# Expert blocks of 32 places instead of 64, with the next block's rows turned behind W2 of the block before

## The reference, cut to what matters

```python
# xt: 1024 tokens x 1024; w1, w3: 32 experts x 1024 x 512; w2: 32 x 512 x 1024
gsel = argmax(xt @ w_group + b_group)             # one of 4 groups of 8 experts
ev, ei = top_k(expert logits of that group, 2)    # two experts a token
ew = softmax(ev) * gprob[gsel]
# the 2048 (token, expert) pairs are sorted by expert
y = (silu(xb @ w1[e]) * (xb @ w3[e])) @ w2[e]     # for the rows xb of each expert e
out = sum over a token's two experts of ew * y
```

## Time and profile before

| | |
|---|---|
| median of 3 runs | 1649.77 us |
| the profiled execution | 1650.04 us |
| its span (first to last instruction) | 1648.4 us |
| mean granted TensorE clock | 0.988 |
| PE busy | 1564.9 us, 95% |
| DVE busy | 560.9 us, 34% |
| ACT busy | 346.8 us, 21% |
| POOL busy | 300.6 us, 18% |
| DMA | 328.42 MB, mean 199 GB/s |

### The profile page before, as it was taken

One profiled execution on the slowest core, in us unless ns is written; L12 is line 12 of the kernel. 1 busy time (PEld: TensorE's weight loads), 2 busy tenths in 40 slices (PEclk: granted clock), 3 DMA queues, 4 the chain that ended last, 5 costly groups with the idle time before them and its releaser, 6 DMA issues.

```text
span 1648.4 us, 21863 instructions
## 1 busy us (share of the span) xinstructions
PE 1564.9 (95%) x7698; PEld 848.1 (51%) x7699; DVE 560.9 (34%) x1542; ACT 346.8 (21%) x859; POOL 300.6 (18%) x431
## 2 busy tenths in 40 slices
PE   7999998999999999998999999799899999999986
PEld 4554544444444444444444555566466666666652
DVE  4210004766566656654222354511011111111115
ACT  3000002443343443433000111111111111111113
POOL 2000001322222222222001001221121212121114
PEclk9999999999999999998999999999999999999997
DMA  9214621553111110103443821699999989999928
GB/s 236 67 56 62 125 78 58 166 181 114 45 32 26 45 33 26 46 13 90 161 136 103 357 107 74 235 416 419 419 419 418 386 352 407 416 421 417 415 85 306
DMA packets 135914, 328.42 MB, mean 199 GB/s; under 512 B 40046, under 2 KB 80398, under 8 KB 126640
## 3 DMA queue, kind: packets, MB, share of 16 engines
q1 hardware_dynamic: 117472, 297.98, 49.5%
q0 software_dynamic: 9984, 17.62, 3.2%
q10 hardware_dynamic: 8400, 12.07, 2.1%
HBM read 276.09 MB, written 55.25 MB: 201 GB/s over the span
## 4 chain that ended last, share of the span: by engine, by line
PE 83%; DVE 7%; DMA 5%; issue 2%; ACT 2%; POOL 1%; SPq 1%; POOLq 0%; ACTq 0%; DVEq 0%
PE PS L856 17%; PE PS L707 12%; PE PS L591 11%; PE PS L870 9%; PE PS L745 7%; PE PS L780 7%; PE PS L693 4%; PE PS L654 4%; PE PS L673 4%; PE PS L586 3%; DMA WA<-w 2%; PE PS L833 2%; DMA BA<-hn_d,ids 1%; POOL WA L1532 1%; PE PS L573 1%
## 5 line engine op out<-in xcount | busy, mean ns | idle before, releaser
L707 PE MATMUL PS<-WA 128*128 128x512 f32 x512 | 255.0, 611 | 2.2 <-ACT WA L967 1.6
L856 PE MATMUL PS<-WA,BA 128*64 128x256 f32 x2048 | 227.6, 379 | 2.9 <-DMA WA<-w 1.5
L856 PEld LDWEIGHTS PS<-WA,BA 128*64 128x64 f32 x2048 | 173.9, 137 | 63.9 <-issue 17.3
L591 PE MATMUL PS<-WA,BA 128*128 128x512 f32 x416 | 180.1, 593 | 2.9 <-DVE WA L1090 2.9
L1450 POOL TENSOR_SCALAR BA<-BA,rin,gates 128x640 f32<-128x640 f32 (+7 forms) x128 | 99.6, 781 | 270.8 <-DVE rin L1209 270.8
L1364 DVE SCALAR_TENSOR_TENSOR BA<-BA,PS 128x256 f32<-128x256 f32 x46 | 19.4, 422 | 340.8 <-ACT BA L1029 340.8
L591 PEld LDWEIGHTS PS<-WA,BA 128*128 128x128 f32 x416 | 78.6, 190 | 99.6 <-issue 96.2
L673 PEld LDWEIGHTS PS<-ident,BA 128*128 128x128 f32 x648 | 79.4, 144 | 94.1 <-issue 86.6
L870 PE MATMUL PS<-WA,BA 128*64 128x512 f32 x512 | 116.9, 597 | 9.7 <-DVE BA L1374 8.7
L707 PEld LDWEIGHTS PS<-WA 128*128 128x128 f32 x512 | 84.6, 190 | 78.4 <-issue 67.6
L957 ACT ACTIVATE BA<-PS,ngm 128x640 f32<-128x640 f32 (+7 forms) x128 | 89.9, 702 | 130.5 <-DVE ngm L1187 126.1
(11 more groups left out here) (249 smaller groups left out, 1548.4 us busy)
## 6 DMA issues: line engine op xcount, KB each, us to landing
WA<-w SPq DMA_DIRECT2D x66, 2048.0 KB, 25.3
BA<-w SPq DMA_DIRECT2D x30, 2048.0 KB, 27.6
rows_d<-WA SPq DMA_DIRECT2D x8, 2048.0 KB, 9.5
rows_d<-BA ACTq DMA_DIRECT2D x92, 128.0 KB, 6.8
WA<-w_in SPq DMA_DIRECT2D x16, 512.0 KB, 5.6
gates_d<-WA SPq DMA_DIRECT2D x32, 256.0 KB, 2.4
WA<-gates_d SPq DMA_DIRECT2D x8, 1024.0 KB, 5.4
BA<-w_in SPq DMA_DIRECT2D x26, 256.0 KB, 6.1
```

The lines of the kernel that those rows point to most:

```text
L591: mm = pe.matmul(PS[:, j % 4, :], ws[:, c % 6, k, :], hnT[:, k, 512 * h:512 * h + 512], start=(k == 0), stop=(k == KT - 1))
L707: mm = pe.matmul(PS[:, 6, :], gw[:, j, k, :], hnT[:, k, 512 * hf:512 * hf + 512], start=(k == 0), stop=(k == KT - 1))
L856: mm = pe.matmul(PS[DH * h:DH * h + DH, bank, 0:256], xT[:, k, :], w[par][:, k, 256 * h:256 * h + 256], start=(k == 0), stop=(k == KT - 1))
```

## The change

`SLOTS` is 32 instead of 64, and an expert has at least 2 blocks (of 32) instead of 1 (of 64). The total is rounded up to an even number, because ACT, DVE and POOL now handle blocks in pairs (`side` 0 and 1). The parts:

- W1 and W3 run in four column groups of 32: two for the halves of W1, two for those of W3, all in bank 0, one after the other in the innermost loop. They share one semaphore, `mm13`. W2 runs in four column groups with 256 output columns each.
- The order on TensorE: W1 and W3 of block b, W2 of block b - 1 (`put_out`), the transposes of the rows of block b + 1 (`next_rows`), the transpose of the hidden rows of block b (`turn_hidden`). The first block of an expert is written apart from its loop, since its `put_out` uses the weights of the expert before.
- The gather brings 32 whole rows into 32 partitions of one of two buffers (`rows_in`). DVE spreads them over 128 partitions with four copies (`spread_rows`), so that two transposes turn them.
- Row numbers are read two blocks ahead, one DMA a block instead of two; the table holds token numbers instead of half-row numbers.
- ACT copies the output in four pieces and stores it with one DMA a block, from one of two buffers.
- The first two blocks' numbers both come from `first_rows`; `mark`, its matmuls and the gather behind them are gone. The first block's rows are turned by 8 transposes straight from the gathered rows.

```diff
-SLOTS = 64
-MAXB = NE + 2 * SEQ // SLOTS
+SLOTS = 32
+MAXB = 2 * NE + 2 * SEQ // SLOTS - 4
+FIRST = 2 * SLOTS
...
# SP
-                sp.wait_ge(S[("mm1", "mm3", "y_ps")[j]], used)
+                sp.wait_ge(S[("mm13", "mm13", "y_ps")[j]], used)
...
# TensorE
-            for m in range(TT):
-                for c in range(2):
-                    for h in range(2):
-                        mm = pe.matmul(PS[DH * h:DH * h + DH, 2, 0:2], mark[:, m, c, :], tok[:, h, m, :], ...)
         def turn_rows():
-            for c in range(4):
+            for c in range(2):
                 mm = pe.transpose(PS[:, 7, P * c:P * c + P], xin[:, P * c:P * c + P], ident[:, :])
...
+        def hidden_sums(b, par, landed):
+            pe.wait_ge(S["xT_evac"], pe.snap(b + 1))
+            for n in range(2):
+                pe.wait_ge(S[f"we{3 * par + n}"], landed)
+            for k in range(KT):
+                for q in range(4):
+                    w = (W1, W3)[q // 2][par]
+                    mm = pe.matmul(PS[SLOTS * q:SLOTS * q + SLOTS, 0, 0:256], xT[:, k, :],
+                                   w[:, k, 256 * (q % 2):256 * (q % 2) + 256], start=(k == 0), stop=(k == KT - 1))
+            mm.then_inc(S["mm13"], 1)
+        def next_rows(b):
+            pe.wait_ge(S["x_free"], pe.snap(b + 2))
+            turn_rows()
+        def put_out(n_done, par, landed):
+            pe.wait_ge(S["hT_done"], n_done)
+            pe.wait_ge(S["y_evac"], n_done)
+            pe.wait_ge(S[f"we{3 * par + 2}"], landed)
+            for j in range(2):
+                for h in range(2):
+                    for n in range(4):
+                        mm = pe.matmul(PS[SLOTS * n:SLOTS * n + SLOTS, 3, 0:256],
+                                       hT[:, FIRST * j + SLOTS * h:FIRST * j + SLOTS * h + SLOTS],
+                                       W2[par][:, 2 * h + j, 256 * n:256 * n + 256], ...)
+            mm.then_inc(S["y_ps"], 1)
+        def turn_hidden(b):
+            pe.wait_ge(S["hid_done"], pe.snap(b + 1))
+            pe.transpose(PS[:, 2, 0:P], hv, ident[:, :]).then_inc(S["hT_ps"], 1)
+        def expert(e, lo, par, landed, landed_before):
+            hi = pe.value_load(starts_i[0:1, bass.ds(e + 1, 1)], ...)
+            hidden_sums(lo, par, landed)
+            if landed_before is not None:
+                put_out(lo, (par - 1) % NW, landed_before)
+            next_rows(lo)
+            turn_hidden(lo)
+            with pe.Fori(lo + 1, hi) as b:
+                hidden_sums(b, par, landed)
+                put_out(b, par, landed)
+                next_rows(b)
+                turn_hidden(b)
+            return hi
...
# ACT
         def gate_and_rows(b):
-            act.wait_ge(S["mm1"], b + 1)
-            nc.scalar.activation(th[:, :], PS[:, 0, 0:256], ACT.Tanh, scale=0.5)...
-            act.wait_ge(S["x_tr"], b + 3)
-            act.wait_ge(S["mm3"], b + 1)
+            act.wait_ge(S["mm13"], b + 1)
+            nc.scalar.activation(th, PS[0:FIRST, 0, 0:256], ACT.Tanh, scale=0.5)...
+            act.wait_ge(S["x_tr"], b + 1)
             nc.scalar.copy(xT_out, xT_ps).then_inc(S["xT_evac"], 1)
+        def put_rows(n_done, side, first):
+            act.wait_ge(S["y_ps"], n_done)
+            for n in range(4):
+                y = nc.scalar.copy(ysb[side][:, 256 * n:256 * n + 256], PS[SLOTS * n:SLOTS * n + SLOTS, 3, 0:256])
+            y.then_inc(S["y_evac"], 1)
+            act.wait_ge(S["y_evac"], n_done + 1)
+            act.dma_start(rows_d[bass.ds(first, SLOTS), :], ysb[side]).then_inc(S[f"y_st{side}"], 16)
+        with act.Fori(1, act.snap(total - 1), 2) as b:
+            for n in range(2):
+                gate_and_rows(act.snap(b + n + 1))
+                act.wait_ge(S[f"y_st{1 - n}"], act.snap(b * 8 + 8 + 16 * n))
+                put_rows(act.snap(b + n + 1), 1 - n, act.snap((b + n) * SLOTS))
...
# DVE
-        step(dve.tensor_scalar(nblk_i, cnt_i, 6, None, ALU.arith_shift_right))
-        step(dve.tensor_scalar(sums[0][:, 16:48], nblk_i, 1, None, ALU.max))
+        step(dve.tensor_scalar(nblk_i, cnt_i, 5, None, ALU.arith_shift_right))
+        step(dve.tensor_scalar(sums[0][:, 16:48], nblk_i, 2, None, ALU.max))
...
+        def spread_rows(side):
+            for q in range(4):
+                rows = dve.tensor_copy(xin[SLOTS * q:SLOTS * q + SLOTS, :], rows_in[side][:, 256 * q:256 * q + 256])
+            rows.then_inc(S["x_free"], 1)
...
+        with dve.Fori(0, total, 2) as b:
+            for side in range(2):
+                now = dve.snap(b + side)
+                hidden(now)          # mm13, tanh: the product, then two halves of 64 partitions
+                dve.wait_ge(S[f"x_blk{side}"], dve.snap(b * 8 + 32))
+                dve.wait_ge(S["x_tr"], dve.snap(b + side + 1))
+                spread_rows(side)
+                take_hidden(now)     # one copy of 128 columns
...
# POOL
+        def load_ids(side, row):
+            pool.dma_start(ids[0:SLOTS, side:side + 1], ids_d[bass.ds(row, SLOTS), 0:1], ...)
+        with pool.Fori(2, total + 2, 2) as b:
+            for side in range(2):
+                pool.wait_ge(S[f"ids_in{side}"], pool.snap(b * 8))
+                pool.wait_ge(S["x_free"], pool.snap(b + side - 1))
+                pool.wait_ge(S[f"x_blk{side}"], pool.snap(b * 8))
+                ...
+                g.indirect_dma_start(rows_in[side], None, hn_d[:, :], ...)
+                load_ids(side, pool.value_load(block_row_i[0:1, bass.ds(b + side + 2, 1)], ...))
```

More of the change, by code:

```diff
@@ L248, in build @@
     ZPARTS = 8
+    ZROWS = MAXB * SLOTS * D // (512 * P)
     steps_at, tile_done_at = [], {}
@@ L875, in _ @@
-        with pe.Fori(0, NE // NW) as e3:
+        def hidden_sums(b, par, landed):
+            pe.wait_ge(S["xT_evac"], pe.snap(b + 1))
+            for n in range(2):
+                pe.wait_ge(S[f"we{3 * par + n}"], landed)
+            for k in range(KT):
+                for q in range(4):
[3 more added lines that the diff above has]
+            mm.then_inc(S["mm13"], 1)
@@ new lines, in next_rows @@
+        def next_rows(b):
[8 more added lines that the diff above has]
+                    for n in range(4):
+                        mm = pe.matmul(PS[SLOTS * n:SLOTS * n + SLOTS, 3, 0:256], hT[:, FIRST * j + SLOTS * h:FIRST * j + SLOTS * h + SLOTS],
+                                       W2[par][:, 2 * h + j, 256 * n:256 * n + 256],
+                                       start=(j == 0 and h == 0), stop=(j == 1 and h == 1))
+            mm.then_inc(S["y_ps"], 1)
@@ L876, in _ @@
+        end = pe.snap(pe.value_load(starts_i[0:1, 0:1], min_val=0, max_val=0))
+        for e in range(NW):
+            end = expert(e, end, e, 16, None if e == 0 else 16)
+        with pe.Fori(1, NE // NW) as e3:
+            end = pe.value_load(starts_i[0:1, bass.ds(e3 * NW, 1)], min_val=2, max_val=MAXB)
             for par in range(NW):
-                expert(e3 * NW + par, e3 + 1, par)
+                end = expert(e3 * NW + par, end, par, pe.snap(e3 * 16 + 16), pe.snap(e3 * 16 if par == 0 else e3 * 16 + 16))
@@ L878, in _ @@
+        end = pe.value_load(starts_i[0:1, NE - NE % NW:NE - NE % NW + 1], min_val=2, max_val=MAXB)
         for e in range(NE - NE % NW, NE):
-            expert(e, e // NW + 1, e % NW)
+            end = expert(e, end, e % NW, 16 * (e // NW + 1), 16 * ((e - 1) // NW + 1))
+        put_out(end, (NE - 1) % NW, 16 * ((NE - 1) // NW + 1))
         pe.wait_ge(S["loop_left"], 1)
@@ L1285, in place @@
                 dve.wait_ge(S["first_ps"], 1)
-                dve.tensor_scalar(ids[:, 2:3], PS[:, 0, 0:1], PS[:, 0, 1:2], None, ALU.add).then_inc(S["first_ids"], 1)
+                for n in range(2):
+                    rows = slice(SLOTS * n, SLOTS * n + SLOTS)
+                    dve.tensor_scalar(ids[0:SLOTS, 2 + n:3 + n], PS[rows, 0, 0:1], PS[rows, 0, 1:2], None, ALU.add) \
+                        .then_inc(S["first_ids"], 1)
             step(dve.tensor_reduce(slot_f[:, m, :], pick, X, ALU.add))
@@ L1500, in _ @@
         scatter_ids(TT - 1)
[L1501 to L1504 removed]
         pool.wait_ge(S["scattered"], 16 * 2 * TT)
[L1507 to L1511 removed]
+        def load_ids(side, row):
+            pool.dma_start(ids[0:SLOTS, side:side + 1], ids_d[bass.ds(row, SLOTS), 0:1],
+                           allow_slow_non_contiguous=True).then_inc(S[f"ids_in{side}"], 16)
```

210 lines of the change are left out of this document (80 added, 130 removed).

## The result

The changed kernel takes 1659.9 us (median of 3 runs, 1659.83 to 1661.95), the kernel before 1649.77: a ratio of 1.0065, 95% interval 1.0051 to 1.0078. It is slower by 0.65%; the forecast was 1622.0 us, 1.7% faster. The profiled execution has a span of 1657.9 us at a mean clock of 0.975.

What follows compares the result with a forecast made beforehand. TensorE set the loop, with the weights' stream close behind as the next wall. From 1650.0 us, 29 off the loop, 0.5 off before it and 0.9 more after gave 1621, stated as 1622; range 1606 to 1656.

Steps and rivals of the forecast that it cites:

- The stream of weights: In the expert loop, 199.5 MB at 414.5 GB/s take 481 us, so the last W2 lands at about 1549.
- except at the start ... I count 1 us: At the loop's start, the third block's numbers wait for the row table: 1 us; first weight slot free at 1067.
- the 2 us that I had put in: In the loop, 2 us added for the granted clock falling after TensorE's waits.
- 78 blocks, the last eight experts among them: Loop count: 78 blocks of 32 instead of 46 of 64; the last eight experts need 22 blocks.
- W1 and W3 four abreast: In each block, 64 instructions in four column groups run four at 0.216 us: 3.45 us, last sum at 3.61.
- the rivals of the groups: In W1, W3 and W2, four column groups don't run abreast: 1700 to about 2000 us; chance 0.16, loads included.
- of the loads: Rival in the column-group matmuls: weight loads can't hide, a block takes 9.5 us, about 1840 us; chance 0.02.
- The chain of ACT and DVE under W2 of the block before: In each block, hidden rows are ready at 5.03 us, covered by the previous block's W2 until 5.18; period 6.4 us.
- The rival of the handshakes: In each block, waits before W1 and late rows cost more: period 7.0 to 7.3 us, 1640 to 1665; chance 0.09.
- The first block 0.5 us earlier: Before the loop, marks and 32 small matmuls go, rows' landing sets ACT's copy: 0.5 us earlier taken.
- Waits of some 4 us for weights, a share of DMA at 1.0 until 1550 and a granted clock under 1.00: Signs of a right forecast in the loop: such waits with most two-block experts, and the low clock in these stretches.
- The stream runs faster: Rival for the loop's weight stream: fewer small packets worth 2% of the rate, 9 us less, 1612; chance 0.09.

Runs made afterwards that it cites:

- Experiment 4: The changed kernel with each loop gather's 32 whole rows put into partitions 0, 4, ..., 124 (1627.7 us) or 0, 2, ..., 62 (1656.8 us).
- experiment 5: The kernel before with each loop gather split into two of 64 half rows, into partitions 0 to 63 and 64 to 127: 1672.4 us, ratio 1.0145.
- Experiment 6: The changed kernel with the last row-number scatter moved earlier (1660.2 us), or the third expert's W2 (1657.8) or W3 and W2 (1653.9) held for the third block's rows.
- e11: The changed kernel with rows gathered into partitions 0, 4, ..., 124 and the third expert's W3 and W2 held until the third block's rows landed: 1621.8 us.
- e1: The changed kernel without the gathers of rows from the third block on: 1614.3 us, ratio 0.9788.
- e4: The changed kernel with GpSimd's last scatter of row numbers put before the second of the two first gathers: 1660.2 us, ratio 1.0059.
- e9: The changed kernel with the third expert's W3 and W2 issued only when the third block's rows have landed: 1653.9 us, ratio 1.0021.
- e2: The changed kernel with rows gathered as quarters of 1 KB into 128 partitions instead of 32 whole rows into 32: 1632.3 us, ratio 0.9895.
- e5: The changed kernel with each loop gather's 32 whole rows put into partitions 0, 4, ..., 124 instead of 0 to 31: 1627.7 us, ratio 0.9864.

## Why the prediction was wrong

The step that failed is "The stream of weights": 199.5 MB at the 414.5 GB/s of the earlier trace rows. I took a rate measured in the kernel before as a property of the transfers, and carried it over a change of the gathers' destination. It had 128 partitions to write and got 32. At 393 GB/s the same 199.5 MB take 508 us, 26 us more. Experiment 4 shows the cause by one changed line, experiment 5 by the gathers alone in the kernel before. That the row gathers keep the weights' transfers waiting is shown by the share of q1 and by the packets, 0.75 us instead of 0.62 (experiment 4); how the partitions are tied to the path is not to be seen in a trace. A rule that fits stands in the Trainium skill (SBUF — State Buffer, section "Door 1: The DMA port swizzle"): bits 4 to 2 and bit 6 of a partition's number choose one of 16 ports, so partitions 0 to 31, 0 to 63 and 0, 2, ..., 62 all reach the same 8, and 0, 4, ..., 124 all 16. All runs here agree with it: 390 to 398 GB/s for the first three, 420 to 422 for the last. The section speaks of the bandwidth of the transfer itself, here 8 MB of rows; what it cost was the rate of the weights beside them. The same skill (DMA: Bandwidth & Descriptors, "Back-pressure in remote DMA") says that a clogged port stalls the other queues of the engine that writes to it. It says so of transfers between cores; the packets here fit it for one core's own, but no trace shows the stall itself.

The second failed term is small in the text: "except at the start ... I count 1 us". The first slot was free at 1074.7, not 1067: 7.7 us. I had the latencies of small transfers behind full queues (7.4 and 8.0 us) and used them inside the loop only; and I did not ask what stands behind DVE's wait for rows. Experiment 6 gets 6 us of it back.

26 + 7.7 = 34 of the 39 us between the forecast loop end (1574) and the measured one (1612.9). Over the whole stream, 1075 to 1580 us, the rate was 391, which makes it 29 + 7.7 = 37; the other 2 are open. With both causes removed the time is 1621.8 us. That it agrees with 1622.0 so well is in part luck: that run's rate is 421, not 414.5, worth 8 us, so something else in the loop is 8 us longer than I worked out. Its trace says where. The last eight experts start at 1426.8, after 4.36 us of waiting for weights; by the sum at 421 GB/s these are there at about 1421. And the 22 blocks from there, with the last W2, take 147.1 us and not 144: one W1 and W3 at a low clock takes 6.33 us instead of 3.66, two waits that the trace puts down to nothing take 1.9 and 1.4, and the first block of an expert mostly comes 0.3 us late. Over the loop the clock costs more than the 2 us that I had put in: L843 is busy for 206.0 + 89.5 = 295.5 us in e11 where 78 x 3.66 are 285.5. But only 2.7 of these 10 us lie in the last 22 blocks, where TensorE sets the time. Why the weights of the last eight come 6 us later than by the sum stays open.

The other steps:
- 78 blocks, the last eight experts among them: right.
- W1 and W3 four abreast: right, 3.66 us for 3.61, so the rivals of the groups and of the loads (slower) fall. The rule of the Trainium skill (TensorE: Matmul & The Clock Gate, "Part 3: Packing small matmuls — row/col tiling") that weight loads overlap running matmuls only where the row group differs went with 1840 us in the prediction. The trace disagrees with it: 64 loads of 114 ns lie within those 3.66 us.
- The chain of ACT and DVE under W2 of the block before: right. Period 6.22 us for 6.4, ACT's copy L1050 as the last releaser, its wait 0.35 us. The rival of the handshakes falls.
- DVE's spreading: 1.18 us, inside 0.8 to 1.7, and free; ACT's four copies 1.49 for 1.5.
- The first block 0.5 us earlier: can't be told. The loop began at 1049.12 for 1050.42, but among the profiled runs of variants that change nothing ahead of it the same point moves by 5 us (1048.7 in e11, 1054.1 in e1).
- Waits of some 4 us for weights, a share of DMA at 1.0 until 1550 and a granted clock under 1.00 were named as what would show the forecast right. All came, and said nothing of the rate: I should have named GB/s. Neither sign of being wrong came, a period over 7 us or a share well under 1.0.
- The rival of the stream looked one way only. "The stream runs faster" got 0.09; that it might run slower had no case and no chance, though its price per GB/s stood in the sum: 1.2 us each, and the forecast gain of 28 us is gone at 24 GB/s less, 390.

The chances followed: 0.20 for slower, all of it on TensorE. The half about TensorE, with all its detail, was right, and it decided nothing once the bound had moved.

## What to carry to other kernels

When a change hands the bound from an engine to the transfers, the rate of the transfers has to be costed like an instruction: list every transfer that runs beside the stream, and ask for each whether its destination, partition by partition, changes. Small gathers that land in partitions 0 to 31 or 0 to 63 took 6% off the rate of the weights in flight beside them; the same rows over all 128 partitions, or one in every four, took 1% or nothing. And a small transfer on the path (scatter, numbers, rows) that meets megabytes of prefetch took 8 us instead of under 4. To put it first in the queue only made the next small transfer late (e4); holding the prefetch until all of them were through got 6 us back (e9).

## What the runs showed of the hardware that was not expected

- Matmuls of 32 columns of weights and 256 columns of data in four column groups: 64 instructions with their 64 loads in 3.66 us, against 7.11 for 64 in two groups. Four abreast cost nothing over two.
- A gather of 0.13 MB a block, about 4% of the bytes, into partitions 0 to 31 or 0 to 63 slows the weights, 92% of the DMA engines' time, by 6%, and the row stores out to memory not at all. The share of DMA stays at 1.02; only GB/s shows it.
- 64 destinations (0 to 63) are no better than 32 (0 to 31): 390 to 393 against 391 to 396 GB/s.
- Spaced destinations are even better than 1 KB quarters over all partitions: 420 to 422 against 414 to 416 GB/s. The row numbers' reads, four columns a block instead of one, may be the reason (q0 has 5.3% of the engines' time in e2 and 4.3% in e5); that was not tried.
- A scatter of row numbers took 7.8 us to land beside 4 MB of loads, 8.3 beside 2 MB, and 2.1 without. GpSimd waited 8.4, 8.9 and 2.7 us for it.
